# Three layer norms of a decoder step: the variance summed with tokens on partitions, four blocks scaled at a time, the shift on ScalarE, the output stored from inside the last norm, and a last column slice of 360

## The reference

```
x <- LN1(alpha*x + 0.5*SwiGLU_1(x))
x <- LN2(alpha*x + W_o [DSA_heads(x) | GDN_heads(x)])
x <- LN3(alpha*x + 0.5*SwiGLU_2(x))

def layer_norm(x, g, b):
    mu = jnp.mean(xf, -1, keepdims=True)
    var = jnp.mean(jnp.square(xf - mu), -1, keepdims=True)
    return (xf - mu) * lax.rsqrt(var + LN_EPS) * g + b

def swiglu(x, w_gate, w_up, w_down):
    return (jax.nn.silu(x @ w_gate) * (x @ w_up)) @ w_down
```

## Time and profile before

| | us |
|---|---|
| median of 3 runs (3201.76 to 3205.47) | 3201.98 |
| the profiled execution | 3202.78 |
| its span, first to last instruction | 3201.1 |
| TensorE busy (matmuls), 90% of the span | 2871.0 |
| VectorE busy, 47% | 1498.0 |
| ScalarE busy, 27% | 874.5 |
| mean granted TensorE clock | 0.949 |

### The profile page before, as it was taken

The page is one execution under the profiler, slowest core; times in us unless marked ns, Lnnn a source line. Parts: engine busy times, 40 slices in busy tenths (PEclk is TensorE's granted clock), DMA queues, the critical chain, the costliest instruction groups (busy, mean ns, idle before and its releaser), DMA issues. The chain is left out here.

```text
span 3201.1 us, 44582 instructions
## 1 busy us (share of the span) xinstructions
PE 2871.0 (90%) x17444; PEld 2602.4 (81%) x17444; DVE 1498.0 (47%) x2359; ACT 874.5 (27%) x1391; POOL 197.5 (6%) x369
## 2 busy tenths in 40 slices
PE   7999999999869999677888487879699999999996
PEld 6999999999668799643887254559499999999994
DVE  3232232233555778558887676441523223333235
ACT  2111111111213467512454244441231111111112
POOL 0000000000000000132000000750000000000000
PEclk9999999999989999859999699999899999999998
DMA  3111111110031122333000200862021111111101
GB/s 118 40 46 46 46 39 46 46 39 26 23 92 41 55 69 75 108 85 89 27 28 8 94 1 5 238 196 96 14 66 47 41 46 41 46 41 41 47 14 56
DMA packets 265832, 185.68 MB, mean 58 GB/s; under 512 B 62847, under 2 KB 245327, under 8 KB 265654
## 3 DMA queue, kind: packets, MB, share of 16 engines
q1 hardware_dynamic: 214902, 115.75, 12.7%
q0 software_dynamic: 20064, 56.23, 5.3%
q10 hardware_dynamic: 30688, 11.27, 1.3%
HBM read 156.97 MB, written 26.22 MB: 57 GB/s over the span
## 5 line engine op out<-in xcount | busy, mean ns | idle before, releaser
L356 DVE TENSOR_TENSOR ffn_hidden<-ffn_hidden,ffn_ps_b 128x1092 f32<-128x1092 f32 x44 | 56.9, 1293 | 400.4 <-PE ffn_ps_b L84 400.4
L310 ACT ACTIVATE ffn_h_hi<-ffn_hidden 128x1092 fp32r<-128x1092 f32 x44 | 49.2, 1119 | 496.8 <-DVE ffn_hidden L356 496.8
L295 ACT ACTIVATE ffn_hi_d<-ffn_raw_d 128x1024 fp32r<-128x1024 f32 x40 | 42.5, 1062 | 495.0 <-PE ffn_ps_b L84 379.0
L84 PE MATMUL ffn_ps_a<-mixer_mix_hi,ffn_hi_g 128*128 128x364 f32 x528 | 117.9, 332 | 25.0 <-DVE ffn_lo_g L339 21.2
L303 ACT ACTIVATE ffn_hidden<-ffn_ps_a 128x1092 f32<-128x1092 f32 x44 | 47.6, 1083 | 290.2 <-PE ffn_ps_a L84 290.2
L84 PE MATMUL ffn_ps_a<-first_x_hi,ffn_hi_g 128*128 128x364 f32 x528 | 117.8, 331 | 5.6 <-DVE ffn_lo_g L339 5.6
L196 POOL DMA_DIRECT2D ffn_raw_d<-in_ffn_w_down x40 | 21.3, 532 | 1586.2 <-DVE ffn_lo_d L345 1400.5
L84 PE MATMUL ffn_ps_a<-first_x_lo,ffn_hi_g 128*128 128x364 f32 x528 | 117.6, 331 | 0.0
L84 PE MATMUL ffn_ps_a<-first_x_hi,ffn_lo_g 128*128 128x364 f32 x528 | 117.5, 331 | 0.0
L84 PE MATMUL ffn_ps_a<-mixer_mix_lo,ffn_hi_g 128*128 128x364 f32 x528 | 117.2, 330 | 0.0
L84 PE MATMUL ffn_ps_a<-mixer_mix_hi,ffn_lo_g 128*128 128x364 f32 x528 | 117.1, 330 | 0.0
(11 more groups left out here) (597 smaller groups left out, 6925.5 us busy)
## 6 DMA issues: line engine op xcount, KB each, us to landing
ffn_raw_d<-in_ffn_w_down POOLq DMA_DIRECT2D x40, 512.0 KB, 3.7
proj_raw<-in_w_in SPq DMA_DIRECT2D x22, 512.0 KB, 3.8
second_ffn_raw_g<-in_ffn_w_gate SPq DMA_DIRECT2D x22, 512.0 KB, 4.1
second_ffn_raw_u<-in_ffn_w_up SPq DMA_DIRECT2D x22, 512.0 KB, 3.7
first_ffn_raw_g<-in_ffn_w_gate SPq DMA_DIRECT2D x21, 512.0 KB
first_ffn_raw_u<-in_ffn_w_up SPq DMA_DIRECT2D x21, 512.0 KB, 3.7
scratch_qkv<-proj_stage POOLq DMA_DIRECT2D x12, 544.0 KB, 3.0
delta_cur<-scratch_qkv SPq DMA_DIRECT2D x8, 768.0 KB, 5.8
```

Of the source, the lines that this page charges most:

```text
L84: last = pe.matmul(out[:, s, 0:SL], w(k), x(k)[:, s * SL:(s + 1) * SL], start=start and n == 0 and p == 0, stop=stop and n == len(ks) - 1 ...
L295: act.activation(d_hi[:, k, :], raw["d"][:, :], ACT.Copy).then_inc(whi_done["d"], 1)
L310: act.activation(h_hi[:, par, fb, :], act_buf[:, fb, :], ACT.Copy).then_inc(hhi_done, 1)
L356: dve.tensor_tensor(hid, hid, ps_b[:, :, 0:SL], ALU.mult).then_inc(mul_done, 1)
```

## The change

- `three_pass` computes 360 columns in the third slice instead of 364 (`USED`); the four pad columns of each PSUM result are set to zero once at the start of a stage (`pads_set`), and TensorE waits for that.
- The norm's variance has tokens on the partitions: the squares become the stationary operand and one column of the 1/1024 matrix the moving one, 3 groups of up to 128 tokens with 8 matmuls each (`variances`). Root and reciprocal then work on 128x3. VectorE multiplies the identity by the three columns of reciprocals (`spread`), and three matmuls of ones with these diagonals bring them to all partitions (`broadcast`), into the slice of `mean` that has been used by then.
- VectorE multiplies four blocks at a time by the broadcast value (`scale`, 2 instructions a slice). ScalarE applies gain and bias, 8 instructions a slice (`shift`), and makes four blocks' high halves in one instruction. VectorE's `low` also takes four blocks at a time.
- The residual that ln1 writes has the bias in it, and is written after `shift`; the bias is no longer added in `mixer_output` and ffn2.
- ln3 turns, copies and stores the tokens itself, half a tile at a time with 3 PSUM buffers and 3 row buffers, between its slices. `store_tokens` is gone.

```diff
 def three_pass(...):
-                last = pe.matmul(out[:, s, 0:SL], w(k), x(k)[:, s * SL:(s + 1) * SL],
+                last = pe.matmul(out[:, s, 0:USED[s]], w(k), x(k)[:, s * SL:s * SL + USED[s]],
...
 def norm(...): TensorE
+            def variances(i):
+                pe.wait_ge(s["squared"], i + 1)
+                if i >= 2:
+                    pe.wait_ge(s["std_done"], i - 1)
+                for j, (at, w) in enumerate(parts):
+                    for k in range(KT):
+                        last = pe.matmul(var[0:w, i % 2, j:j + 1], sq[:, i % 2, k, at:at + w], ones_mean[:, 0:1],
+                                         start=k == 0, stop=k == KT - 1)
+                last.then_inc(s["var_done"], 1)
+            def broadcast(i):
+                pe.wait_ge(s["spread_made"], i + 1)
+                pe.wait_ge(s["centred"], i + 1)
+                for j, (at, w) in enumerate(parts):
+                    last = pe.matmul(mean[:, i, at:at + w], ones[0:w, :], spread[0:w, i % 2, j, 0:w],
+                                     start=True, stop=True)
+                last.then_inc(s["broadcast_done"], 1)
...
             means(0)
-            for i in range(SLICES):
-                if i + 1 < SLICES:
-                    means(i + 1)
-                pe.wait_ge(s["squared"], i + 1)
-                for k in range(KT):
-                    last = pe.matmul(var[:, i, 0:SL], ones_mean[:, :], sq[:, i % 2, k, :],
-                                     start=k == 0, stop=k == KT - 1)
-                last.then_inc(s["var_done"], 1)
+            means(1)
+            variances(0)
+            broadcast(0)
+            means(2)
+            variances(1)
+            broadcast(1)
+            variances(2)
+            if store is not None:
+                turn(0)
+            broadcast(2)
+            if store is not None:
+                turn(1)
+                turn(2)
 ScalarE
+            def shift(i, h):
+                act.wait_ge(s["squared"], i + 1)
+                act.wait_ge(s["scaled"], 2 * i + h + 1)
+                for k in range(4 * h, 4 * h + 4):
+                    act.activation(res[:, k, cols[i]], res[:, k, cols[i]], ACT.Identity, scale=gb[:, 0, k:k + 1],
+                                   bias=gb[:, 1, k:k + 1]).then_inc(s["made"], 1)
+                if x_hi is not None:
+                    act.wait_ge(s["made"], KT * i + 4 * h + 4)
+                    act.activation(x_hi[:, 4 * h:4 * h + 4, cols[i]], res[:, 4 * h:4 * h + 4, cols[i]], ACT.Copy
+                                   ).then_inc(s["hi_done"], 1)
...
 VectorE
+            centre(0)
+            centre(1)
+            invert(0)
+            scale(0)
+            centre(2)
+            low(0, 0)
+            low(0, 1)
+            invert(1)
+            scale(1)
+            copy(0)
+            low(1, 0)
+            invert(2)
+            scale(2)
+            low(1, 1)
+            copy(1)
+            low(2, 0)
+            low(2, 1)
+            copy(2)
```

More of the change, by code:

```diff
@@ L31 @@
 SL = 364
+USED = (SL, SL, NT - 2 * SL)
 TP = SLICES * SL
@@ L199, in _ @@
         def _(sp):
-            if resid_b is not None:
-                column_load(sp, shift[:, :], resid_b[0], shift_in)
             with sp.Fori(1, FB) as n:
@@ L404, in norm @@
         cols = slices(SLICES)
+        last_slice = [((t + 1) * P - 1 if t < TILES - 1 else NT - 1) // SL for t in range(TILES)]
         @block.sync
@@ L417, in _ @@
                 early(sp, s["early_in"])
+            if store is not None:
+                y_prompt, y_sample = store
+                for t in range(TILES):
+                    w = tile_width(t)
+                    dst = (y_prompt[0, t * P:(t + 1) * P, :] if t < TILES - 1
+                           else y_sample.rearrange("b t d -> (b t) d"))
+                    sp.wait_ge(s["copied"], 2 * t + 2)
+                    sp.dma_start(dst, rows[0:w, t % 3, :]).then_inc(s[f"out_done{t % 3}"], 16)
+                for r in range(3):
+                    sp.wait_ge(s[f"out_done{r}"], 16 * ((TILES - r + 2) // 3))
         @block.tensor
@@ new lines, in broadcast, with turn @@
+            def broadcast(i):
[5 more added lines that the diff above has]
+                last.then_inc(s["broadcast_done"], 1)
+            def turn(i):
+                for t in range(TILES):
+                    if last_slice[t] != i:
+                        continue
+                    w = tile_width(t)
+                    pe.wait_ge(s["made"], KT * (i + 1))
+                    for half in range(2):
+                        n = 2 * t + half
+                        if n >= 3:
+                            pe.wait_ge(s["copied"], n - 2)
+                        for k in range(4):
+                            last = pe.transpose(turned[0:w, n % 3, k, :], res[:, half * 4 + k, t * P:t * P + w],
+                                                ident[:, :])
+                        last.then_inc(s["turned_done"], 1)
@@ L461, in _ @@
             act.wait_ge(s["gb_in"], 32)
-            high(0)
-            for i in range(1, SLICES):
-                if i + 1 < SLICES:
-                    square(i + 1)
-                root(i)
-                high(i)
+            shift(0, 0)
+            shift(0, 1)
+            square(2)
+            root(1)
+            shift(1, 0)
+            root(2)
+            shift(1, 1)
+            shift(2, 0)
+            shift(2, 1)
         @block.vector
@@ L487, in low @@
-            def low(i):
-                for k in range(KT):
-                    dve.wait_ge(s["hi_done"], KT * i + k + 1)
-                    dve.wait_ge(s["normed"], KT * i + k + 1)
-                    dve.scalar_tensor_tensor(x_lo[:, k, cols[i]], res[:, k, cols[i]], gb[:, 1, k:k + 1],
-                                             x_hi[:, k, cols[i]].bitcast(F32), ALU.add, ALU.subtract)
+                dve.reciprocal(rstd[:, i, :], rstd[:, i, :]).then_inc(s["inverted"], 1)
+                dve.wait_ge(s["inverted"], i + 1)
@@ new lines, in invert, with scale @@
+                if i >= 2:
+                    dve.wait_ge(s["broadcast_done"], i - 1)
+                dve.tensor_tensor(spread[:, i % 2], ident[:, :].unsqueeze(1).to_broadcast([P, len(parts), P]),
+                                  rstd[:, i, :].unsqueeze(2).to_broadcast([P, len(parts), P]), ALU.mult
+                                  ).then_inc(s["spread_made"], 1)
+            def scale(i):
+                dve.wait_ge(s["broadcast_done"], i + 1)
+                dve.wait_ge(s["squared"], i + 1)
+                dve.wait_ge(s["centred"], i + 1)
+                for h in range(2):
+                    r = res[:, 4 * h:4 * h + 4, cols[i]]
+                    dve.tensor_tensor(r, r, mean[:, i, 0:SL].unsqueeze(1).to_broadcast([P, 4, SL]), ALU.mult
+                                      ).then_inc(s["scaled"], 1)
@@ new lines, in low, with copy @@
+            def low(i, h):
+                if x_hi is not None:
+                    dve.wait_ge(s["hi_done"], 2 * i + h + 1)
+                    dve.wait_ge(s["made"], KT * i + 4 * h + 4)
+                    x = slice(4 * h, 4 * h + 4)
+                    dve.tensor_tensor(x_lo[:, x, cols[i]], res[:, x, cols[i]], x_hi[:, x, cols[i]].bitcast(F32),
+                                      ALU.subtract)
+            def copy(i):
+                for t in range(TILES):
+                    if store is None or last_slice[t] != i:
+                        continue
+                    w = tile_width(t)
+                    for half in range(2):
+                        n = 2 * t + half
+                        dve.wait_ge(s["turned_done"], n + 1)
+                        if t >= 3:
+                            dve.wait_ge(s[f"out_done{t % 3}"], 16 * (t // 3))
+                        dve.tensor_copy(rows[0:w, t % 3, half * 512:half * 512 + 512].rearrange(
+                            "p (k f) -> p k f", k=4), turned[0:w, n % 3, :, :]).then_inc(s["copied"], 1)
@@ L3085, in decoder_step @@
                 ffn(nc, "ffn2", a["ffn2_w_gate"], a["ffn2_w_up"], a["ffn2_w_down"], res, mix_hi, mix_lo,
[L3086 removed]
+                    raws, weigh=True)
             with nc.cleanup_on_exit():
[L3088 to L3090 removed]
+                norm(nc, "ln3", a["ln3_g"], a["ln3_b"], ident, ones, ones_mean, res, None, None,
+                     store=(out["y_prompt"], out["y_sample"]))
 _INS = ["x_prompt", "x_sample", "cache_k", "cache_v", "cache_kidx", "state_gdn", "state_conv", "page_table",
```

122 lines of the change are left out of this document (34 added, 88 removed).

## The result

The changed kernel takes 3209.47 us (median of 20 runs, 3198.12 to 3218.80), the kernel before 3204.52 us in the same session (20 runs, 3198.88 to 3208.91). The ratio is **1.0019, 95% interval 1.0012 to 1.0027**: some 6 us slower, just inside the 0.2% that the prediction called "same". (Its bound in microseconds, 3208.4, was worked out from a median before of 3202, and lies 1.1 us under the result.) The profiled execution took 3208.57 us with a span of 3206.9, against 3202.78 and 3201.1.

The account below looks back on a forecast made before the run. TensorE was taken to bound the ffns, a chain through four engines the norms. Norms +8.8, columns -6.7 and residual bias -0.4 gave +1.7 us on 3202.8, 3204.5; with the median 0.8 lower, 3204 was forecast, range 3190 to 3213.

Parts of the forecast that it names:

- The narrower third slice: Matmuls of the third slice: 4032 of them lose 4 columns at 0.417 ns each, -6.7 us (bounds 0 and -7.4).
- `mixer_output`'s -0.4: ScalarE's scaling of the residual loses its bias and gives back TensorE's wait behind it, -0.4 us.
- The norms, +8.8 us: ln1, ln2 and ln3 with its store, the lower clock included: 193.5 us against 184.7, +8.8 us.
- the stepped chain: ln1's four engine queues stepped instruction by instruction at traced durations; last `low` ends at 51.7 us, before 0.5 is taken off.
- the end of variance(0) +1.4 (0 to 3): In each norm, the lower clock slows the end of the first variance, 4.9 us at full clock, by 1.4 us.
- The norm at full clock: Norms stepped without a clock loss: ln1 53.8, ln2 51.2, ln3 58.4, together 163.4 us.
- the clock's price, +30.1: Loss to TensorE's lower clock in the norms: +9.1 us in ln1, the same in ln2, +11.9 in ln3.
- The clock stays up: Rival: norms keep the full clock, kernel 3176 us; 3190 if it falls in one gap only; chance 0.20 for both.
- The columns give nothing: Rival: the weight load sets the 166 ns a matmul, so only the norms' loss stands, 3211 us; chance 0.15.
- The clock falls and stays down: Rival: the clock stays low from variance(0) to each norm's end, TensorE's 21 us behind it double, 3238 us; chance 0.07.
- the burst of the earlier trace: In `project` before the change, 18 one-column instructions in 2.05 us, after which the clock fell from 1.00 to 0.50.
- the rule that the prediction weighed: Clock follows how busy TensorE was recently; read as busy time, the norms would keep the higher clock, as in the first rival.

Follow-up runs that it names:

- experiment 1: Changed kernel with the variance matmuls given 128 moving columns instead of one: 3189.86 us, ratio 0.9960 to the kernel before.
- experiments 2 and 3: 2: changed kernel with 364 columns in the third slice again, 3218.65 us, 1.0052; 3: kernel before with 360 columns and zeroed pads, 3199.65 us, 0.9988.

## Why the prediction came out

**The time and its sign.** 3204 was forecast with a range of 3190 to 3213; it is 3209.5, and the likeliest outcome, "within 0.2%", came with 0.19% slower. The ground for it, a small gain of columns set against norms that lose to the clock, is what experiments 1 to 3 show. Of the 5.5 us, 2.5 are the kernel before, whose median was 3202.0 when the forecast was made and 3204.5 beside the result. In the traces the change came to +5.8 us where +1.7 was forecast: 6 us more in the norms, 2 less in the rest, and the 2 are within the scatter of the middle. That the total came so close is in part luck, since inside the norms two errors offset each other, as shown below.

**The narrower third slice, -6.7 us.** Right within what can be told: -3.8 and -10.6 in the two pairs of runs. The traces have -2.7, -1.5, -4.9 and -4.2 us for an ffn, where -2.6 was forecast. `mixer_output`'s -0.4 and the zeroed pads are too small to be seen.

**The norms, +8.8 us.** As the prediction counts them: ln1 63.4 (forecast 62.9), ln2 63.0 (60.3), ln3 73.1 (70.3), +14.8 in all. ln1 followed the stepped chain nearly to the microsecond: the last `low` ends 60.6 us from the first matmul, and 51.7 - 0.5 + 9.1 = 60.3 was forecast. The term that was mis-sized is "the end of variance(0) +1.4 (0 to 3)": the clock fell earlier in it in ln2 and ln3, and it took 8.80 and 8.53 us against the 4.9 + 1.4 of the sum, 2.5 and 2.2 us more than taken and outside the bound. Those two make 4.7 of the 6. How early it falls differs from trace to trace: in the twelve norms with one column variance(0) took 5.94 to 8.95 us.

**"The norm at full clock", 163.4 us, and the clock's price, +30.1.** The first was too low by 3.5 to 4 us a norm. With 128 columns the three norms take 177.6 us as the prediction counts them, 174.6 without ln1's slow first means. The clean case is ln2 of experiment 1, at 0.99: 54.7 us where the stepping gave 51.2. The changed kernel's ln2 takes 63.0, so there the clock is worth 8.3 us, against 9.1 forecast, and in ln3 11.0 against 11.9; as 128 columns cost 0.4 to 0.7 us a variance themselves, both are about right. In ln1 the difference is only 2.6 us (5.6 without the first means), because experiment 1 itself ran there at the low clock in part; so the three norms' 22.0 us (25 without those means) is a lower bound of the clock's price, and it does not show 30.1 to be wrong. The fit of ln1 is the luck: its base was too low as well, and the clock cost less there than the 9.1 taken; its variance(0), at 6.02 us, was slowed least of the three.

What was low in the base is the shift, for one. It was taken at 0.5 us each. Its row says 677 ns of duration, and eight in a row take 4.76 us in ln3 (a window of the kernel after):

```profile
3158.00:3166.00 8.00, 8.00 (x39) 5.80 (x37) 5.03 (x3) 4.76 (x8) 0.00 (x0) 0.87 0.00 0
```

That is 0.595 each, just under the upper bound of 0.6, and 0.4 us more for every four, some three times on the path of a norm. The Trainium skill (ScalarE: Activation LUTs, What ACT_TABLE_LOAD costs) gives 93 ns for each per-partition operand on top of 186 + 0.833 a column. By that an estimate for one shift is 675 ns; the trace agrees to 2 ns. The variances at 5.5 us instead of 4.9 are the price of 128 columns; the remaining us or two a norm are waits of the four-engine chain that I did not separate.

**The rivals.** "The clock stays up" was priced at 3176. When it was kept up in most of the norms, the kernel took 3190; it needed the early table load and the shorter tail to come to 3174 to 3179. "The columns give nothing" fell with experiments 2 and 3. "The clock falls and stays down" did not come: the clock rose again inside the full matmuls of means(2) (0.68 in their window, 0.79 in the next).

**A reading of the rows.** The rival "the clock stays up" counted for itself that the burst of the earlier trace rows was "followed by other short work". It was followed by instructions of 512 columns on 64 partitions, and the clock fell at 1088.0 inside the first of them, not inside the burst:

```profile
1087.61 2.40 PE L771 MATMUL proj_spare<-main_ki_t,proj_shared 64*128 64x512 f32 x4
```

So the earlier trace rows by themselves did not show that the one-column burst was the cause; experiment 1 does, for the norm.

**Busy and the clock.** TensorE is busy for 11.15 of 11.30 us at 0.50 in the window from 872.70; with the same loads and 128 columns its clock was 1.00 while it was busy for less of the time (5.99 of 7.00 us). So the busy time of the profile does not foretell the level here. By the rule that the prediction weighed, from the Trainium skill (TensorE: Matmul & The Clock Gate, What's actually happening), read as busy time, the first of these windows would have been at the high clock; the trace disagrees.

## What to carry to other kernels

A matmul with one moving column is not free when the weights are the data: it costs its weight load (0.107 us an instruction here), and in these norms TensorE's clock fell during or behind a run of them, which the next stages paid for. Try more (even useless) columns for such a reduction if full matmuls follow on the critical path; here 128 were worth 19 us, and numbers between 1 and 128 were not tried. Look for a table load between a short TensorE stage and its consumer: 1.28 us was on the path three times, a one-element call in idle time moved it off, and with the shorter wait TensorE kept its clock. And before moving work off VectorE, step the chain for the engine that becomes the end: here it was ScalarE's per-partition shifts, then VectorE again.

## What the runs showed of the hardware that was not expected

- In these norms 48 instructions of 128 columns took 5.5 us (6.9 to 7.1 where the clock fell), and of one column 5.8 to 9.7, although at 1.00 the one-column ones take 0.107 us each, 5.1 for 48: the short form is the slower one, since it ran in part or wholly at the lower level.
- GpSimd beside VectorE: a 128x384 multiply on VectorE went from 0.56 to 1.96 us, and in ln2 to 3.36, while GpSimd ran a 128x1456 subtraction.
- The first means of a norm (32 instructions of 364 columns) took 10.05, 11.75 or 13.07 us behind the same 3.1 us of idle time, in kernels with the same code up to there but for the table load, and 10.03 or 11.72 behind 2.2 us. With it a single trace of a norm is uncertain by some 3 us, and the kernel's own runs spread over 20 us (3198.12 to 3218.80), so that terms of 3 us were settled by rows and not by medians.
